# A two-block transformer on one core: a changed order of the forgetting attention's projections and a moved norm factor

## The reference

```python
def rmsnorm(x, g):
    xf = x.astype(jnp.float32)
    y = xf * lax.rsqrt(jnp.mean(xf * xf, axis=-1, keepdims=True) + RMS_EPS)
    return (y * g.astype(jnp.float32)).astype(x.dtype)

h = rmsnorm(x, norm_mix)
proj = h @ w_in
q_a, k_a, v_a, f_a, q_b, kv_b, g_b, gate_a, gate_b = jnp.split(proj, ...)
log_f = jax.nn.log_sigmoid((f_a + b_forget).astype(jnp.float32)).transpose(0, 2, 1)
o_a = fox_attention(q_a, k_a, v_a, log_f)      # scores also get ci - c, the running sums of log_f
```

## Time and profile before

| | us |
|---|---|
| median of 3 runs (2943.07 to 2945.43) | 2944.6 |
| the profiled execution's own time | 2943.07 |
| its span, first to last instruction | 2941.0 |
| PE busy / DVE busy / ACT busy | 2802.5 / 1451.4 / 1078.4 |
| mean granted TensorE clock | 0.968 |

### The profile page before, as it was taken

How to read it: one execution, slowest core, us unless ns; L and a number is a source line. 1 busy time by engine, 2 the same in 40 slices (tenths; PEclk the granted TensorE clock), 3 DMA queues, 4 the chain that set the end, 5 groups by cost and what they waited for, 6 DMA issues and landing times.

```text
span 2941.0 us, 35031 instructions
## 1 busy us (share of the span) xinstructions
PE 2802.5 (95%) x14040; PEld 2338.8 (80%) x14040; DVE 1451.4 (49%) x2464; ACT 1078.4 (37%) x1905; POOL 14.6 (0%) x29
## 2 busy tenths in 40 slices
PE   5789999998899999999799999999998899999998
PEld 5678888887788888878688888888787788888886
DVE  6764434357644343566464444243656554453343
ACT  3353222234533222454353343143454442342231
POOL 1000000000000000000000000000000000000000
PEclk9899999998899999999699999999999799999999
DMA  4102333221022333222102323323213013323231
GB/s 125 53 1 86 105 92 97 93 89 57 1 86 91 96 101 100 83 65 82 48 1 86 107 79 108 93 93 101 69 51 117 6 37 93 101 93 108 91 103 58
DMA packets 186148, 231.42 MB, mean 79 GB/s; under 512 B 11794, under 2 KB 140148, under 8 KB 185988
## 3 DMA queue, kind: packets, MB, share of 16 engines
q1 hardware_dynamic: 184436, 225.95, 24.6%
q0 software_dynamic: 976, 1.32, 0.3%
q10 hardware_dynamic: 576, 1.92, 0.2%
HBM read 227.05 MB, written 2.11 MB: 78 GB/s over the span
## 4 chain that ended last, share of the span: by engine, by line
PE 85%; DVE 10%; ACT 3%; issue 2%; SPq 0%; DMA 0%; DVEq 0%; ACTq 0%
PE bank L534 24%; PE bank L536 24%; PE bank L535 24%; PE bank L696 4%; PE bank L681 2%; DVE Wl L1841 1%; PE bank L752 1%; PE bank L751 1%; PE bank L931 1%; PE bank L631 1%; PE bank L762 1%; PE bank L747 0%; DVE TMP L2023 0%; DVE Hl L1888 0%; PE bank L1133 0%
## 5 line engine op out<-in xcount | busy, mean ns | idle before, releaser
L1841 DVE TENSOR_TENSOR Wl<-RAW,Wh 128x1024 fp32r<-128x1024 f32 (+1 forms) x430 | 509.1, 1209 | 375.1 <-ACT Wh L1232 374.5
L1232 ACT ACTIVATE Wh<-RAW 128x1024 fp32r<-128x1024 f32 (+1 forms) x430 | 435.5, 1039 | 401.9 <-PE bank L536 401.6
L534 PE MATMUL bank<-Hh,Wh 128*128 128x512 f32 (+1 forms) x976 | 385.9, 395 | 2.6 <-DVE Hl L1888 2.6
L536 PE MATMUL bank<-Hh,Wl 128*128 128x512 f32 (+1 forms) x976 | 381.0, 390 | 0.0
L535 PE MATMUL bank<-Hl,Wh 128*128 128x512 f32 (+1 forms) x976 | 381.0, 390 | 0.0
L534 PE MATMUL bank<-Wh,A 128*128 128x512 f32 x864 | 337.2, 390 | 0.0
L536 PE MATMUL bank<-Wh,A 128*128 128x512 f32 x864 | 336.3, 389 | 0.0
L535 PE MATMUL bank<-Wl,A 128*128 128x512 f32 x864 | 336.2, 389 | 0.0
L534 PE MATMUL bank<-HA,Wh 128*128 128x512 f32 x704 | 274.7, 390 | 0.8 <-DVE HA L1888 0.8
L536 PE MATMUL bank<-HA,Wl 128*128 128x512 f32 x704 | 274.0, 389 | 0.0
L535 PE MATMUL bank<-HA,Wh 128*128 128x512 f32 x704 | 273.9, 389 | 0.0
(11 more groups left out here) (355 smaller groups left out, 4126.5 us busy)
## 6 DMA issues: line engine op xcount, KB each, us to landing
RAW<-in_w_up_dram SPq DMA_DIRECT2D x108, 512.0 KB, 3.8
RAW<-in_w_down_dram SPq DMA_DIRECT2D x108, 512.0 KB, 3.8
RAW<-in_w_in_dram SPq DMA_DIRECT2D x90, 512.0 KB, 3.8
RAW<-in_w_gate_dram SPq DMA_DIRECT2D x44, 512.0 KB, 3.9
RAW<-in_w_out_dram SPq DMA_DIRECT2D x32, 512.0 KB, 3.8
RAW<-in_cmp_w_dram SPq DMA_DIRECT2D x16, 512.0 KB, 3.9
RAW<-in_w_o_fox_dram SPq DMA_DIRECT2D x8, 512.0 KB, 3.4
RAW<-in_w_o_nsa_dram SPq DMA_DIRECT2D x8, 512.0 KB, 3.4
```

Source lines behind the costliest of these rows:

```text
L534: pe.matmul(o, sh, mh, start=first, stop=False)
L536: return pe.matmul(o, sl, mh, start=False, stop=last)
L1232: sc.activation(M.Wh[:, v % NHL, 0:n], M.RAW[:, v % NRAW, 0:n], ACT.Copy).then_inc(G.w_hi, 1)
L1841: ve.tensor_tensor(M.Wl[:, v % NHL, 0:n], M.RAW[:, v % NRAW, 0:n], M.Wh[:, v % NHL, 0:n].bitcast(F32), ALU.subtract).then_inc(G.w_lo, 1)
```

## The change

- The second block's projections are made in the order q, forget and gate columns, k, v (before: k, forget and gate columns, q, v), in the weight plan and in all three programs.
- For k, ACT raises the semaphore of the high parts once, after the last of its four copies, and DVE waits for that once ahead of its four subtractions (before: once for each copy, and a wait ahead of each subtraction).
- In DVE's `factor_side` four yields stand ahead of `factor`, and one behind it, where five stood behind it. The total stays.
- SNK and BF get words of their own instead of the end of SS, and the area behind the fixed tiles is no longer rounded up to 128 bytes: it starts at byte 141216 of a partition instead of 141184, so every tile in it (A, HA, QA, KAh, KAl, VF and others) moves by 32 bytes.

```diff
-        for c in (2, 3, 0, 1):
-            if c == 0:
+        for c in range(4):
+            rows(w, IN2_Q + c * 256, 256, KD, 4)
+            if c == 1:
                 plan.append([(f, 0, KD, 8, 32), (g, 8, KD, 24, 32)])
-            rows(w, IN2_Q + c * 256, 256, KD, 4)
...
+        self.SNK = fixed("SNK", [12])
...
+        self.BF = fixed("BF", [2])
...
-        self.SNK, self.BF = self.SS[:, 48:60], self.SS[:, 60:62]
-        self.ar = (self.next + 127) // 128 * 128
+        self.ar = self.next
...
         for c in range(2):
-            lin_t(f"fk{l} {c}", KD, M.Hh, M.Hl, normed(n) if c == 0 else None)
+            lin_t(f"fq{l} {c}", KD, M.Hh, M.Hl, normed(n) if c == 0 else None)
...
-            lin_t(f"fq{l} {c}", KD, M.Hh, M.Hl)
+            lin_t(f"fk{l} {c}", KD, M.Hh, M.Hl)
...
                     for r in (0, 64):
-                        sc.activation(M.KAh[r:r + 64, 4 * c + 2 * j + x, :], M.OS[64 * x:64 * x + 64, j, :], ACT.Copy).then_inc(*hi.up())
+                        i = sc.activation(M.KAh[r:r + 64, 4 * c + 2 * j + x, :], M.OS[64 * x:64 * x + 64, j, :], ACT.Copy)
+                i.then_inc(*hi.up())
...
     def factor_side(n):
+        for _ in range(4):
+            yield
         factor(n, slice(0, NT))
-        for _ in range(5):
-            yield
+        yield
         if n in BY_TOKEN:
             yield
...
+                ve.wait_ge(*hi.due())
                 for x in range(2):
                     h = 4 * c + 2 * j + x
                     for r in (0, 64):
-                        i = lower(M.KAl[r:r + 64, h, :], M.OS[64 * x:64 * x + 64, j, :], M.KAh[r:r + 64, h, :])
+                        i = ve.tensor_tensor(M.KAl[r:r + 64, h, :], M.OS[64 * x:64 * x + 64, j, :], M.KAh[r:r + 64, h, :].bitcast(F32), ALU.subtract)
```

More of the change, by code:

```diff
@@ L1647, in evac @@
                     for r in (0, 64):
-                        sc.activation(M.KAh[r:r + 64, 4 * c + 2 * j + x, :], M.OS[64 * x:64 * x + 64, j, :], ACT.Copy).then_inc(*hi.up())
+                        i = sc.activation(M.KAh[r:r + 64, 4 * c + 2 * j + x, :], M.OS[64 * x:64 * x + 64, j, :], ACT.Copy)
+                i.then_inc(*hi.up())
             return evac
         for c in range(2):
-            lin_t(f"fk{l} {c}", KD, fox_k(c), normed(n) if c == 0 else None)
+            lin_t(f"fq{l} {c}", KD, fox_q(c), normed(n) if c == 0 else None)
         next_unit()
@@ L1655, in scalar_program @@
         for c in range(2):
-            lin_t(f"fq{l} {c}", KD, fox_q(c))
+            lin_t(f"fk{l} {c}", KD, fox_k(c))
         lin_s(f"fv{l}", KD, keep(lambda s: M.VF[:, s, :], n))
@@ L2478, in evac @@
             def evac(j, name):
-                ve.wait_ge(G.fox_lo, fox_lo.n - 1)
+                if c:
+                    ve.wait_ge(G.fox_lo, fox_lo.n - 1)
                 by_token(M.OS[:, j, :], name, n, 0.125)
@@ L2488, in evac @@
             def evac(j, name):
-                if c:
-                    ve.wait_ge(G.fox_lo, fox_lo.n - 1)
+                ve.wait_ge(G.fox_lo, fox_lo.n - 1)
                 by_token(M.OS[:, j, :], name, n)
+                ve.wait_ge(*hi.due())
                 for x in range(2):
```

## The result

The changed kernel takes 3020.8 us in the median of 4 runs (3016.95 to 3022.2), against 2943.8 for the kernel before on the same chip: a ratio of 1.0261, 95% interval 1.0243 to 1.0279. It is 77 us slower. I had forecast 2990 us and a range to 3003, so the sign was right and the size was not: about 30 us were missing.

A forecast was written before the change was run, and what follows sets the result against it. PE, busy 95% of the span, was taken as the bound. Norms 21.3 + projections 18.9 + clock 6.8 = 47.0 us on 2943.07 gave 2990 us, range 2978 to 3002, or 2965 to 3003 with two rivals.

The forecast's parts named there:

- The layout: All area tiles, moved by 32 bytes: taken as 0 us for all engines; PE could gain or lose a few us.
- rival 4: Area tiles: shifted operands slow PE by 1% or more, 28 us on top, 3018 us; chance 0.04.
- The norms: All eight norms: the factor chain behind four yields makes PE wait; 21.3 us in sum.
- norms 1, 3, 4 and 6: PE waits 4.0 us at the rb transposes; net 3.6 each at 1 and 3, 3.5 each at 4 and 6.
- norm 2: PE's rb transposes ahead of a lin_s with smaller units: a wait of 1.6 us.
- norms 5 and 7: No rb, but piece 7 stands behind the chain: net 1.65 us each, 3.3 together.
- norm 0: DVE is the bound there: it wins 0.5 us and pays 2.64 later, costing 2.2.
- The projections: Second block, q before k: two waits for Wl less the forget-column gain, 9.45 us per layer, 18.9 for two.
- wait for FGT: PE's wait for the forget columns, 1.05 us in each layer, goes away with q's lighter banks ahead.
- The first wait: PE at v's first unit waits 6.3 us for Wl in each layer.
- The second wait: PE at v's third unit waits 4.2 us for Wl in each layer.
- The clock: PE behind six new waits of 4.0 to 4.2 us: lower clock after four, 1.7 us each, 6.8 in sum.

## Why the prediction was wrong in size

**The layout: the step that failed.** I took 0 for all engines "by that nearest row", two rows of DVE. The experiments put +31.5 us in its place (the layout alone): 6.5 ns on each of 5472 matmuls, 2.9% of their spacing. For DVE and ACT the 0 held. The row was of another engine, and of a tile one word off, while what slows PE is visible only in PE's own starts. The mechanism stood in rival 4, with a chance of 0.04 and the words "nothing either" for and against; that its 28 us are near the 31.5 is luck, as they are 1% of all of PE's busy time and the cost is 2.9% on part of the matmuls. With no row for a case the bound had to be wider: already 1% on some 5500 matmuls of 0.23 us is 13 us, and even a range with that end (3016) would have missed 3020.8. The last sentence of the prediction did name the sign that came: matmuls of A and HA that last longer than those of Hh. Without the layout the change costs 40.3 us (35.6 to 44.7), against my 47.0, so the other terms together were some 7 us too high.

**The norms: right.** At norms 1, 3, 4 and 6 rb waited 3.9 us (forecast 4.0), at norm 2 1.55 (1.6). At norms 5 and 7 piece 7 held PE 2.35 us where piece 6 had held it 0.80, net 1.55 (1.65). (The sum of the prediction gives a wait of 2.45 there; the 2.6 among its signs was a slip.) At norm 0 the waits for rb and CS sum to 2.85 + 7.84 = 10.7, against 8.7 before, +2.0 (2.2). This term is the least firm: with norm 0 as before the wait on CS is 8.1 to 9.5 us from kernel to kernel. PE comes past it at 67.92 us instead of 66.16, 1.8 later (65.5 to 66.4 in the other kernels with norm 0 as before). Sum 4 x 3.9 - 1.8 + 1.55 + 3.1 + 2.0 = 20.5, forecast 21.3. For the norms alone the time rose by 25.0 (20.0 to 29.7), the clock being in it.

**The projections: right in the cause, too high in the second wait.** No wait for FGT is left; KAl starts 2.63 us behind OS's end. DVE and PE of the changed kernel in layer 0:

```profile
1317.06 2.79 DVE L2499 TENSOR_TENSOR KAl<-OS,KAh 64x512 fp32r<-64x512 f32 x4 [2.63 <-ACT KAh L1649]
...
1321.38 1.21 DVE L1843 TENSOR_TENSOR Wl<-RAW,Wh 128x1024 fp32r<-128x1024 f32 x1
...
1336.47 4.63 DVE L1843 TENSOR_TENSOR Wl<-RAW,Wh 128x1024 fp32r<-128x1024 f32 x4
```

```profile
1322.64 0.80 PE L535 MATMUL bank<-Wh,Hh 128*128 128x512 f32 x1 [5.97 <-DVE Wl L1843]
1337.75 0.50 PE L535 MATMUL bank<-Wh,Hh 128*128 128x512 f32 x1 [1.22 <-DVE Wl L1843]
```

The first wait is 5.97 (forecast 6.3), in both layers. From the first Wl to the third DVE takes 15.1 us (forecast 1296.6 - 1281.37 = 15.2). The second wait is 1.2 us in layer 0 and 2.5 in layer 1, not 4.2: behind the first the clock fell, and v's two units took PE 1336.53 - 1322.64 = 13.9 us instead of 11.0. I had written that this loss is taken back from the wait behind it, and it was; but I kept the second wait at 4.2 and counted it among the waits behind which the clock may fall. In layer 0 lower clock and wait together are 1.2 + (13.9 - 11.0) = 4.1 us, so counting the wait whole was right for the sum, and giving it a clock loss of its own (up to 2 x 1.7) was not. In layer 1 it is 2.5 + (12.6 - 11.0) = 4.1. So the term is 5.97 + 4.1 - 1.05 = 9.0 a layer by the trace, 18.0; the order alone cost 15.0 (10.6 to 19.4), against my 18.9.

**The clock: about right in size, by a different set of waits, and so in part by luck.** Windows of PE in the changed kernel, behind the waits at norm 1, on CS at norm 2, at norm 5, on the second Wl of layer 1, and at norm 7 (from:to, us, busy, granted clock):

```profile
282.90:287.90 5.00, 4.96 (x17) 0.66 0.01 3
...
681.30:686.30 5.00, 5.00 (x26) 1.00 0.23 59
...
1786.20:1791.20 5.00, 5.00 (x16) 0.69 0.00 0
...
2214.30:2219.30 5.00, 5.00 (x22) 1.00 0.77 233
...
2658.20:2663.20 5.00, 5.00 (x15) 0.66 0.01 3
```

Behind the waits of 3.9 us, four in a kernel, it fell to the lower level (1.2 instead of 2.4 GHz) every time in the three kernels that have them, mostly to a mean of 0.66 over 5 us, some 1.6 us lost. Behind the second Wl waits (1.2 to 2.5 us) it never did. I took four of these six at 1.7, 6.8 us; it was the four at the norms, 6.4 us. Behind the 2.3 us waits at norms 5 and 7, which I hadn't counted, it fell both times here, once of two without the layout, and not at all with the norms alone. The Trainium skill (TensorE: Matmul & The Clock Gate, section HAM oscillation — how this bites in real kernels) says that a long enough wait makes the work behind it start cold. For the 3.9 us waits the traces agree every time; the shorter ones they show both ways. Against this, the loss behind CS at norm 2 went away in each of the three kernels with all norms moved, while the wait there stayed 2.9 us: about 1.6 us back that I hadn't counted. Of the eleven kernels with norm 2 as before, ten show that loss; in the one with HA alone moved the clock stayed up, so the norms needn't be what decides it. Together that is 6.4 - 1.6 = 4.8 us with the norms alone and, with the two falls at norms 5 and 7, 8.0 in the changed kernel's trace, on either side of the 6.8.

## What to carry to other kernels

When a tile is moved in memory, compare starts of the same matmul a few rows apart, one operand at a time: 7 ns of 227 are easy to overlook and cost 31 us here, beside 40 for all moved instructions together. Here 128-byte multiples for both operands of the large matmuls were worth 1.1%, so keep them, and don't bound an unknown on one engine by a row of another. Where one engine hands four pieces to another, a semaphore for each lets the second start behind the first; one for all added about 2 us to every bank, while the order of the projections by itself cost nothing that the times show.

## What the hardware showed beyond that

- A 512-column fp32r matmul starts 234 ns behind the one before it instead of 227, at the full clock, if either operand starts 32 or 96 bytes behind a multiple of 128. At 64 bytes behind one a streamed operand costs the same (HA 396 ns), a loaded one less than half of it on average (A 391 to 394, starts 229.5 apart). Why both is so isn't settled. Attention's operands moved too; their matmuls are few, and no run here bounds them.
- The clock in the sparse attention isn't the same from one trace to the next, nor from layer to layer. In 60 us from the second wait on KVS, in the two layers, the kernel before had (from:to, us, busy, granted clock)

```profile
1422.30:1482.30 60.00, 51.10 (x254) 0.59 0.03 10
2276.30:2336.30 60.00, 51.20 (x280) 0.65 0.03 9
```

and the kernel with the layout alone 0.77 in its second layer, with 320 PE instructions in the 60 us. No change of this document touches an instruction there. As an estimate from these windows, a granted clock 0.1 higher over 60 us is worth up to 6 us, about the spread between executions of one kernel (2940.4 to 2948.5 for the kernel before); that this stretch makes the spread isn't shown. Before two spans are compared to a few us, it is worth a look.
